# Three stage seams of a decoder step: embedding rows turned tile by tile, the convolution state turned in the decode chain, the layer embeddings loaded and split during the down projection

## The chip, the core and the metric

The kernel runs on one core of a Trainium2 chip. The core has TensorE (matrix products, into PSUM), VectorE, ScalarE and GpSimd (POOL), each with an instruction queue of its own that is worked off in order, and 16 DMA engines; SyncE (SP) issues most DMAs. Engines wait for each other by semaphores. The metric is device time in microseconds of one execution; lower is better.

## The reference

One inference step of a two-layer decoder trunk: 512 prompt tokens and 8 x 4 decode tokens share the weights, in all 544 tokens of width 1024.

```python
def trunk_layer(h, p, pos0, past, weights):
    a = rmsnorm(h, g_attn)
    qa, ka, va, qi, ki, wi, qb, kb, vb, u = split_columns(a @ w_in)
    ...                                   # three head groups: sparse, stick-breaking, pooling
    mix = jnp.concatenate([o_a, o_b.reshape(B, T, WIDTH_B), o_c], axis=-1)
    h = h + mix @ w_out
    y_ffn, new_conv = conv_ffn(rmsnorm(h, g_ffn), conv_prefix, w_up, conv_w, conv_b, w_down)
    h = h + y_ffn
    h = h + jax.nn.sigmoid(rmsnorm(h, g_ple) @ w_ple_gate) * (p @ w_ple_proj)
```

In `conv_ffn`, `f @ w_up` gives a gate and a value half of 2816 columns each; the gate goes through a causal convolution of width 3 over tokens (for decode tokens the two rows before come from `state_conv`), then SiLU, times the value, then `@ w_down`. `p` (256 wide) is a second input per token and layer, the layer embedding.

## The kernel before

Activations are kept with features on the partitions: `hT` is 8 blocks of 128 features by 544 tokens. Weights are streamed in **units** of 128 x 1024 numbers, 106 per layer: 12 and 8 for `w_in`, 8 for `w_out` (U_OUT), 44 for `w_up` (U_UP; gate and value by turns), 24 for `w_down` (U_DOWN, three per output block), 2 for `w_ple_proj` (U_PROJ), 8 for `w_ple_gate` (U_GATE). SP loads a unit into one of four raw buffers (`load_unit`, which waits for `w_lo` of the unit four before), ScalarE rounds it to `w_H` (`split`, which waits for `w_used`, that is, for the unit two before to be used), VectorE makes the rest `w_L` = raw - `w_H` and counts `w_lo`. TensorE then does every product as three (`tri_product`: high x high, low x high, high x low), and `dense` is one unit: 8 blocks of 6 matmuls with 272 token columns each.

`norm_block` on ScalarE makes the rounded, gain-scaled input (`aH` or `bH`) and the square of each hT block, `norm_low` on VectorE the low half (`aL`, `bL`), GpSimd adds up the squares, `square_sum` on TensorE sums them over the partitions with four fp32 matmuls (shown as eight), and `root` on ScalarE takes the inverse root with Ln and Exp, for which it loads tables.

What sets the order is the order in the program of each engine, written by hand. The places at issue:

- **Start.** SP loads the constants `con`, the mask, the page numbers, all four prompt tiles of `x_prompt` in one DMA and then `x_sample` into `xy`, then 12 small vectors, then the first four weight units. TensorE waits for both parts of `xy` and turns the 5 tiles (8 transposes each), VectorE copies them to `hT` (line 1170) and counts `h_new`. Then come the vectors' turn, the splits of two units and the first `norm_block`s.
- **Out to up projection.** `state_conv` is loaded to `st_tok` when the decode chain is done (line 592). After the last out unit TensorE turns it (line 2031, 22 transposes), does `square_sum(1)`, waits for ScalarE's copy to `stT` and enters the loop over up units. ScalarE's queue there holds the last splits and `norm_block(1, 7)`, the copy to `stT`, `root(1)`, and then the loop `ffn`: per gate block `split` of an even unit, the convolution steps, a sigmoid, `split` of the odd unit, and the rounding of the product. VectorE has the steps between; a block's odd unit is thus split only behind most of the convolution of that block.
- **Decode chain.** While VectorE picks the top keys, TensorE turns 16 key pages (line 1917) and forms logits; then it waits for ScalarE's and VectorE's softplus (line 1501) before the stick-breaking sums (line 1979) and the output products (lines 2005, 2016).
- **Down projection to embedding projection.** SP loads `p_tok` when the last down unit is used (line 602). TensorE turns it (line 2070, 10 transposes), ScalarE copies it as `pH`, VectorE makes `pL`, and the 8 blocks of the projection follow, with `square_sum(2)` behind the fourth. ScalarE moves each block to `projT`.

## Time and profile before

| | us |
|---|---|
| median of 3 runs | 1719.51 |
| lowest and highest | 1717.09, 1720.02 |
| the profiled execution | 1722.34 |
| its span in the profile | 1720.5 |
| TensorE busy | 1637.9 (95% of the span) |
| VectorE, ScalarE, GpSimd busy | 885.7, 681.6, 271.3 |
| mean granted clock of TensorE | 0.958 |

The profile is one execution. A granted clock of 1.00 is 2.4 GHz, one of 0.50 is 1.2 GHz. In rows of the timeline, the first number is the start, the second the duration, and the bracket holds the idle time of the engine ahead of the row and what ended it. Matmuls overlap in a pipeline, so the step from one start to the next, not the duration, is the time that one costs.

### The profile page before, as it was taken

The numbers are of one execution on the slowest core, as the hardware profiler recorded it, in microseconds if no ns is written. First come the engines' busy times: TensorE is split into PE (matmuls) and PEld (weight loads), VectorE is DVE, ScalarE is ACT, GpSimd is POOL, SyncE is SP. The second block draws the span as 40 slices with busy tenths as digits, with TensorE's granted clock in tenths as the row PEclk, the third lists the DMA queues.
The fourth block names the chain that finished last, engine by engine and source line by source line (L and its number), as shares of the span: only waits on it lengthen the run. The fifth ranks groups of instructions, "written<-read, shape, count | busy, mean of one in ns | idle before, by whom it ended". The sixth has DMA issues, their size and how long they took to land.

```text
span 1720.5 us, 31176 instructions
## 1 busy us (share of the span) xinstructions
PE 1637.9 (95%) x12030; PEld 1487.6 (86%) x12032; DVE 885.7 (51%) x1567; ACT 681.6 (40%) x981; POOL 271.3 (16%) x448
## 2 busy tenths in 40 slices
PE   5999979999999999998999999799999999999898
PEld 4787836799999999997978786369999999999898
DVE  5657884144555553322748488632355555522325
ACT  3344544235444442224443344532444444322241
POOL 2320240021111111000104105101111111100000
PEclk9999989699999999998999999888999999999989
DMA  5133142132223232332322311322232322233321
GB/s 163 51 95 81 32 134 74 30 86 74 85 85 98 79 89 80 89 92 75 86 75 79 103 48 55 94 66 69 72 89 85 94 85 85 80 92 89 98 61 57
DMA packets 225670, 140.07 MB, mean 81 GB/s; under 512 B 13074, under 2 KB 219684, under 8 KB 225504
## 3 DMA queue, kind: packets, MB, share of 16 engines
q1 hardware_dynamic: 223172, 133.32, 26.9%
q0 software_dynamic: 2400, 5.42, 1.0%
q8 instruction: 65, 1.06, 0.3%
q14 instruction: 33, 0.27, 0.1%
HBM read 131.06 MB, written 7.65 MB: 81 GB/s over the span
## 4 chain that ended last, share of the span: by engine, by line
PE 83%; DVE 10%; ACT 2%; issue 2%; DMA 1%; POOL 0%; DVEq 0%; SPq 0%; POOLq 0%; ACTq 0%
PE ps L1624 24%; PE ps L1626 23%; PE ps L1625 23%; DVE score L1285 2%; DVE m L1282 2%; PE ps L1930 1%; PE ps L2005 1%; PE ps L1687 1%; DVE w_L L1184 1%; PE ps L1773 1%; PE ps L1917 1%; PE ps L1873 1%; PE ps L1927 1%; DVE stat L1403 1%; PE ps L1651 1%
## 5 line engine op out<-in xcount | busy, mean ns | idle before, releaser
L1184 DVE TENSOR_TENSOR w_L<-w_raw,w_H 128x1024 fp32r<-128x1024 f32 (+4 forms) x236 | 257.3, 1099 | 443.7 <-ACT w_H L822 443.7
L1624 PE MATMUL ps<-bH,w_H 128*128 128x272 f32 x1664 | 481.9, 290 | 1.4 <-ACT projT L822 1.4
L1626 PE MATMUL ps<-bH,w_L 128*128 128x272 f32 x1664 | 480.2, 289 | 0.0
L1625 PE MATMUL ps<-bL,w_H 128*128 128x272 f32 x1664 | 478.5, 288 | 0.0
L822 ACT ACTIVATE w_H<-w_raw 128x1024 fp32r<-128x1024 f32 (+4 forms) x236 | 220.0, 943 | 298.6 <-PE ps L1626 298.3
L1624 PEld LDWEIGHTS ps<-bH,w_H 128*128 128x128 f32 x1664 | 313.5, 188 | 2.3 <-ACT projT L822 1.9
L1625 PEld LDWEIGHTS ps<-bL,w_H 128*128 128x128 f32 x1664 | 314.5, 189 | 0.2
L1626 PEld LDWEIGHTS ps<-bH,w_L 128*128 128x128 f32 x1664 | 313.4, 188 | 0.0
L1624 PE MATMUL ps<-actH,w_H 128*128 128x272 f32 x704 | 204.1, 290 | 0.0
L1626 PE MATMUL ps<-actH,w_L 128*128 128x272 f32 x704 | 203.7, 289 | 0.0
L1625 PE MATMUL ps<-actL,w_H 128*128 128x272 f32 x704 | 202.7, 288 | 0.0
L1624 PE MATMUL ps<-aH,w_H 128*128 128x272 f32 x512 | 153.5, 300 | 1.6 <-DVE aL L1190 1.6
L1626 PE MATMUL ps<-aH,w_L 128*128 128x272 f32 x512 | 149.4, 292 | 0.0
L1625 PE MATMUL ps<-aL,w_H 128*128 128x272 f32 x512 | 148.8, 291 | 0.0
L1625 PEld LDWEIGHTS ps<-actL,w_H 128*128 128x128 f32 x704 | 132.7, 189 | 0.0
L1624 PEld LDWEIGHTS ps<-actH,w_H 128*128 128x128 f32 x704 | 132.5, 188 | 0.0
L1626 PEld LDWEIGHTS ps<-actH,w_L 128*128 128x128 f32 x704 | 132.4, 188 | 0.0
L1624 PEld LDWEIGHTS ps<-aH,w_H 128*128 128x128 f32 x512 | 98.0, 191 | 14.1 <-issue 12.2
L1624 PE MATMUL ps<-w_H,aH 128*128 128x512 f32 (+5 forms) x240 | 92.8, 387 | 8.5 <-DVE aL L1196 4.9
L1625 PEld LDWEIGHTS ps<-aL,w_H 128*128 128x128 f32 x512 | 98.2, 192 | 0.0
L1626 PEld LDWEIGHTS ps<-aH,w_L 128*128 128x128 f32 x512 | 97.8, 191 | 0.0
L1625 PE MATMUL ps<-w_L,aH 128*128 128x512 f32 (+5 forms) x240 | 89.9, 375 | 0.0
(318 smaller groups left out, 2427.2 us busy)
## 6 DMA issues: line engine op xcount, KB each, us to landing
w_raw<-in_w_up SPq DMA_DIRECT2D x88, 512.0 KB, 3.8
w_raw<-in_w_down SPq DMA_DIRECT2D x32, 512.0 KB, 3.6
w_raw<-in_w_in SPq DMA_DIRECT2D x24, 512.0 KB, 4.9
w_raw<-in_w_ple_gate SPq DMA_DIRECT2D x16, 512.0 KB, 3.7
w_raw<-in_w_down SPq DMA_DIRECT2D x16, 384.0 KB, 3.2
w_raw<-in_w_out SPq DMA_DIRECT2D x16, 320.0 KB, 3.4
w_raw<-in_w_in SPq DMA_DIRECT2D x8, 452.0 KB, 3.5
w_raw<-in_w_in SPq DMA_DIRECT2D x8, 384.0 KB, 3.2
```

The costliest lines, as they stand in the source:

```text
L822: return act.activation(out, in_, ACT.Copy, scale=scale)
L1184: ins = dve.tensor_tensor(w_L[u % SPLIT][:, a:b], w_raw[raw_slot(l, u)][:, a:b], w_H[u % SPLIT][:, a:b].bitcast(F32), ALU.subtract)
L1282: dve.max(m8[:, :], sc).then_inc(dve_step, steps.step())
L1285: dve.match_replace(sc, m8[:, :], sc, TAKEN).then_inc(dve_step, steps.step())
L1403: dve.tensor_reduce(stat[:, s, 0, :], ps[:, SOFT_BANK[s]:SOFT_BANK[s] + 2, 0:P * (t + 1)], AX.X, ALU.max).then_inc(dve_step, steps.step())
L1624: pe.matmul(out, wh, xh, start=start, stop=False)
L1625: pe.matmul(out, wh, xl, start=False, stop=False)
L1626: return pe.matmul(out, wl, xh, start=False, stop=stop)
L1651: mm = pe.matmul(ps[:, SUM_BANK[i] + half, 0:HALF], mean, x[:, HALF * half:HALF * half + HALF], start=n == 0, stop=n == 1, skip_group_chec ...
L1687: pe.matmul(ps[:, 7, 0:P * (t + 1)], featT[rows, F_QI + e // 2, P * t:P * t + P], featT[rows, F_KI, 0:P * (t + 1)], start=True, stop=True) ...
L1773: pe.matmul(bz(h, i), featT[rows, F_KB + h // 2, P * i:P * i + P], featT[rows, F_QB + h // 2, P * i:TP], start=i != 3, stop=False, skip_gr ...
L1873: mm = pe.matmul(ps[HD * n:HD * n + HD, 4, 0:384], V[:, b, HD * n:HD * n + HD], probT[:, b, n, :, :], start=b == 0, stop=b == t, skip_grou ...
```

## The change

At the start the prompt tiles are loaded by four DMAs with a semaphore each, ahead of the mask, and TensorE waits tile by tile; VectorE casts the mask behind the copies. The load of `state_conv` waits for the last page turn instead of the decode chain's end, its turns stand ahead of the stick-breaking sums, and ScalarE's copy behind its copies of the turned probabilities. The first of the 11 turns of the up loop on TensorE is written out, with `square_sum(1)` behind its first unit. The load of `p_tok` is issued behind the fourth down unit's, its turns stand behind the sixth down block, ScalarE's and VectorE's parts one block later at most, in other PSUM banks and in SBUF that the convolution has left. Two matmuls that wrote zeros to two banks ahead of the down projection are gone.

```diff
-        p_tok = sb("p_tok", [P, TILES, PLE], F32, ple)
-        pH = sb("pH", [P, 2, T], F32R, ple)
-        pL = sb("pL", [P, 2, T], F32R, ple)
...
+        keepT = sb("keepT", [P, KF, 2 + 2 * NB], F32, ffn)
+        late = ExitStack()
+        p_tok = sb("p_tok", [P, TILES, PLE], F32, late)
+        pH = sb("pH", [P, 2, T], F32R, late)
+        pL = sb("pL", [P, 2, T], F32R, late)
+        late.close()
         stT = sb("stT", [P, KF, 2 * NB], F32, ffn)
-        keepT = sb("keepT", [P, KF, 2 + 2 * NB], F32, ffn)
...
+        con_ld, page_ld, con_cast = sg("con_ld"), sg("page_ld"), sg("con_cast")
+        x_ld = [sg(f"x_ld{t}") for t in range(TILES)]
...
-        PP_BANK, PROJ_BANK = [0, 1, 6], [0, 4, 6]
+        PP_BANK, PROJ_BANK = [2, 3, 1], [0, 4, 6]
...
             sp.dma_start(con[:], t_in["con"]).then_inc(con_ld, 16)
-            sp.dma_start(mask[:], t_in["dcon"][:, ND:]).then_inc(con_ld, 16)
+            for t in range(4):
+                sp.dma_start(xy[:, t, :], t_in["x_prompt"][0, P * t:P * t + P, :]).then_inc(x_ld[t], 16)
+            sp.dma_start(xy[0:TS, 4, :], t_in["x_sample"].rearrange("b s d -> (b s) d")).then_inc(x_ld[4], 16)
+            sp.dma_start(mask[:], t_in["dcon"][:, ND:]).then_inc(con_cast, 16)
             sp.dma_start(pages[:], t_in["page_table"].rearrange("b n -> (b n)").rearrange("(o n) -> o n", o=1)).then_inc(page_ld, 16)
-            sp.dma_start(xy[:, 0:4, :], t_in["x_prompt"].rearrange("o (t p) d -> p (o t) d", p=P)).then_inc(x_ld, 16)
-            sp.dma_start(xy[0:TS, 4, :], t_in["x_sample"].rearrange("b s d -> (b s) d")).then_inc(x_ld, 16)
...
-                sp.wait_ge(d_hi, at(d_hi, 2))
+                sp.wait_ge(ik_sc, at(ik_sc, 1))
                 hold(sp)
-                sp.wait_ge(d_lo, at(d_lo, 2))
+                sp.wait_ge(kt_mm, at(kt_mm, NPAGES))
                 hold(sp)
                 sp.dma_start(st_tok[:], t_in["state_conv"][L].rearrange("o b r c -> (o b r) c")).then_inc(st_ld, 16)
...
-                for u in range(U_DOWN, U_PROJ + RAW):
+                for u in range(U_DOWN, U_DOWN + RAW):
                     load_unit(u)
-                sp.wait_ge(w_used, at(w_used, SPLIT + U_PROJ))
+                sp.wait_ge(s_mul, at(s_mul, KF))
+                hold(sp)
+                sp.wait_ge(g_keep, at(g_keep, KF))
                 hold(sp)
                 sp.dma_start(p_tok[:, 0:4, :], t_in["p_prompt"][L].rearrange("o b (t p) c -> p (o b t) c", p=P)).then_inc(p_ld, 16)
                 sp.dma_start(p_tok[0:TS, 4, :], t_in["p_sample"][L].rearrange("o b s c -> (o b s) c")).then_inc(p_ld, 16)
-                for u in range(U_PROJ + RAW, UNITS + (RAW if l + 1 < LAYERS else 0)):
...
+                act.wait_ge(st_tr, at(st_tr, 1))
+                copy(stT[:, :, :], ps[:, 4, 0:KF * 2 * NB].rearrange("p (f b) -> p f b", b=2 * NB)).then_inc(st_ev, 1)
                 act.wait_ge(vp_use, at(vp_use, NPAGES))
...
                     norm_block(1, m)
-                act.wait_ge(st_tr, at(st_tr, 1))
-                copy(stT[:, :, :], ps[:, 5, 0:KF * 2 * NB].rearrange("p (f b) -> p f b", b=2 * NB)).then_inc(st_ev, 1)
                 root(1)
...
+                def p_split():
+
+                    act.wait_ge(pp_tr, at(pp_tr, 1))
+                    for b in range(3):
+                        nt = 2 if b < 2 else 1
+                        src = ps[:, PP_BANK[b], 0:nt * 256].rearrange("p (t k q) -> p k t q", k=2, q=P)
...
+                        ins.then_inc(pp_hi, 1)
+
                 for m in range(KD):
                     for q in range(3):
                         split(U_DOWN + 3 * m + q + 2)
                     norm_block(2, m)
-
-                act.wait_ge(pp_tr, at(pp_tr, 1))
...
-                    ins.then_inc(pp_hi, 1)
+                    if m == 5:
+                        p_split()
+
...
-            dve.wait_ge(con_ld, 32)
+            dve.wait_ge(con_ld, 16)
...
-            dve.tensor_copy(con_bf[:, 1, :], mask[:, 0:P])
-            dve.tensor_copy(con_bf[:, 2, :], mask[:, P:2 * P]).then_inc(con_cast, 1)
             for t in range(TILES):
...
                     ins.then_inc((emb_ev if i < 2 else h_new), 1)
+            dve.wait_ge(con_cast, 16)
+            dve.tensor_copy(con_bf[:, 1, :], mask[:, 0:P])
+            dve.tensor_copy(con_bf[:, 2, :], mask[:, P:2 * P]).then_inc(con_cast, 1)
...
+                    if m == 6:
+                        p_low()
...
-            pe.wait_ge(con_ld, 32)
-            pe.wait_ge(x_ld, 32)
+            pe.wait_ge(con_ld, 16)
             for i in range(2 * TILES):
                 t, b, n = i // 2, i % 2, TOKW[i // 2]
+                if b == 0:
+                    pe.wait_ge(x_ld[t], 16)
                 if i >= 8:
                     pe.wait_ge(emb_ev, i - 7)
                 for k in range(4):
                     mm = pe.transpose(ps[:, i % 8, P * k:P * k + n], xy[0:n, t, P * (4 * b + k):P * (4 * b + k) + P], ident[0:n, 0:n])
                 mm.then_inc(emb_tr, 1)
-            pe.wait_ge(con_cast, 1)
+            pe.wait_ge(con_cast, 17)
...
+                pe.wait_ge(kt_ev, at(kt_ev, NPAGES))
+                pe.wait_ge(st_ld, at(st_ld, 16))
+                hold(pe)
+                for f in range(KF):
+                    mm = pe.transpose(ps[:, 4, 16 * f:16 * f + 16], st_tok[:, P * f:P * f + P], ident[0:16, 0:16])
+                mm.then_inc(st_tr, 1)
...
+                pe.wait_ge(st_ev, at(st_ev, 1))
                 pe.wait_ge(d_lo, at(d_lo, 2))
...
-                pe.wait_ge(st_ld, at(st_ld, 16))
-                pe.wait_ge(h_new, at(h_new, KD + 6))
-                hold(pe)
-                for f in range(KF):
-                    mm = pe.transpose(ps[:, 5, 16 * f:16 * f + 16], st_tok[:, P * f:P * f + P], ident[0:16, 0:16])
-                mm.then_inc(st_tr, 1)
-                square_sum(1)
-                pe.wait_ge(st_ev, at(st_ev, 1))
-                pe.wait_ge(h_new, at(h_new, KD + 7))
-                hold(pe)
-
-                with pe.Fori(0, KF // 2) as i:
+                def up(i, first=False):
+
                     for j in range(4):
                         n = 4 * i + j
                         pe.wait_ge(w_lo, at(w_lo, RAW + U_UP + n + 1))
-                        if j % 2 == 0:
+                        if j % 2 == 0 and not first:
                             pe.wait_ge(v_mul, at(v_mul, 2 * i + j // 2 + 1))
-                        if j == 3:
+                        if j == 3 and first:
                             pe.wait_ge(n_rec, at(n_rec, 2))
-                        dense(2 * j, j, range(KD), bH, bL, True, True, norm_=1 if j == 0 else None).then_inc(w_used, 1)
+                        if first and j < 3:
+                            pe.wait_ge(h_new, at(h_new, KD + (7, 8, 8)[j]))
+                        dense(2 * j, j, range(KD), bH, bL, True, True, norm_=1 if first and j == 0 else None).then_inc(w_used, 1)
+                        if first and j == 0:
+                            square_sum(1)
+
+                up(0, True)
+                with pe.Fori(1, KF // 2) as i:
+                    up(i)
 
                 pe.wait_ge(v_mul, at(v_mul, KF - 2 + 3))
                 hold(pe)
-                for b in range(2, 4):
-                    pe.matmul(ps[:, b, 0:HALF], con_bf[:, 3, :], con_bf[:, :, :].rearrange("p a n -> p (a n)")[:, 0:HALF], start=True, stop=True)
...
-
-                pe.wait_ge(p_ld, at(p_ld, 32))
-                pe.wait_ge(h_new, at(h_new, 3 * KD - 1))
-                hold(pe)
-                for t in range(TILES):
...
+                    if m == 5:
+                        pe.wait_ge(p_ld, at(p_ld, 32))
+                        pe.wait_ge(v_mul, at(v_mul, KF + 2))
+                        hold(pe)
+                        for t in range(TILES):
...
+                                mm = pe.transpose(ps[:, PP_BANK[t // 2], c:c + n], p_tok[0:n, t, P * k:P * k + P], ident[0:n, 0:n])
+                        mm.then_inc(pp_tr, 1)
+
                 pe.wait_ge(g_keep, at(g_keep, KF))
...
                             pe.wait_ge(pr_ev, at(pr_ev, m - 2))
+                        elif m == 0:
+                            pe.wait_ge(h_new, at(h_new, 3 * KD - 1))
                         elif m == 1:
                             pe.wait_ge(h_new, at(h_new, 3 * KD))
                         mm = dense(PROJ_BANK[m % 3], u, range(2), pH, pL, True, True, c0=P * mm_, stride=512)
```

How the instructions stand. TensorE, from the out projection (`aH`, `aL`) to the up projection (`bH`, `bL`), first before, then of the change:

```order
1506 L1626 MATMUL ps<-aH,w_L 128x272
1507 L2031 MATMUL ps<-con,st_tok 128x16 [waits st_ld,h_new]
1508 L2031 MATMUL ps<-con,st_tok 128x16 x21
1509 L1651 MATMUL ps<-r_all,con 128x272 [waits n_add]
1510 L1651 MATMUL ps<-r_all,con 128x272
1511 L1651 MATMUL ps<-a_tmp,con 128x272 [waits n_sq]
1512 L1651 MATMUL ps<-a_tmp,con 128x272
1513 L2038 UNCONDITIONAL_BRANCH [waits st_ev,h_new]
```

```order
1514 L1642 MATMUL ps<-aH,w_L 128x272
1515 L1640 MATMUL ps<-bH,w_H 128x272 [waits a_lo,h_new,w_lo]
...
1562 L1642 MATMUL ps<-bH,w_L 128x272
1563 L1667 MATMUL ps<-r_all,con 128x272 [waits n_add]
1564 L1667 MATMUL ps<-r_all,con 128x272
1565 L1667 MATMUL ps<-a_tmp,con 128x272 [waits n_sq]
1566 L1667 MATMUL ps<-a_tmp,con 128x272
1567 L1640 MATMUL ps<-bH,w_H 128x272 [waits h_new,w_lo]
```

The turns of `st_tok` are gone from here, and a whole unit of 48 matmuls stands between the out projection and the square sum.

TensorE, in the decode chain of the change, between the biased logits (`bias_d`) and the stick-breaking sums (`L_d`):

```order
1097 L1989 MATMUL ps<-bias_d,id_bf 96x288 [waits d_bias]
1098 L1989 MATMUL ps<-bias_d,id_bf 96x288
1099 L1995 MATMUL ps<-con,st_tok 128x16 [waits kt_ev,st_ld]
1100 L1995 MATMUL ps<-con,st_tok 128x16 x21
1101 L2001 MATMUL ps<-L_d,con 128x192 [waits d_sp]
1102 L2002 MATMUL ps<-L_n,con 128x192
```

Here the turns are new; before, the row of `L_d` stood right behind that of `bias_d`.

TensorE, around the turns of `p_tok`, first before (behind the last down unit), then of the change (behind the sixth of eight down blocks), and then where the embedding projection (`pH`, `pL`) begins:

```order
2771 L1626 MATMUL ps<-actH,w_L 128x272
2772 L2070 MATMUL ps<-con,p_tok 128x128 [waits p_ld,h_new]
2773 L2070 MATMUL ps<-con,p_tok 128x128 x7
2774 L2070 MATMUL ps<-con,p_tok 128x32 x2
2775 L1624 MATMUL ps<-pH,w_H 128x272 [waits w_lo,pp_lo,g_keep]
```

```order
2704 L2089 MATMUL ps<-con,p_tok 128x128 [waits p_ld,v_mul]
2705 L2089 MATMUL ps<-con,p_tok 128x128 x7
2706 L2089 MATMUL ps<-con,p_tok 128x32 x2
2707 L1640 MATMUL ps<-actH,w_H 128x272 [waits h_new,w_lo]
...
2970 L1642 MATMUL ps<-actH,w_L 128x272
2971 L1640 MATMUL ps<-pH,w_H 128x272 [waits w_lo,h_new,pp_lo,g_keep]
```

The projection now follows a down matmul directly, and the wait for `p_ld` stands two down blocks ahead of it.

## Rows read from the trace of the kernel before

**Rows 1.** The page, part 4: shares of the chain of waits.
```profile
PE 83%; DVE 10%; ACT 2%; issue 2%; DMA 1%; POOL 0%; DVEq 0%; SPq 0%; POOLq 0%; ACTq 0%
```
**Rows 2.** The chain of waits at the start: start us, us, what.
```profile
2.49 9.65 DMA xy<-in_x_sample
12.27 4.51 PE ps L1614 x20
16.81 2.89 DVE hT L1170 x6
...
25.14 0.79 PE ps L1624
```
**Rows 3.** Timeline, down projection to embedding projection, both layers.
```profile
791.29 0.71 DVE L1556 TENSOR_TENSOR hT<-hT,ps 128x544 f32<-128x544 f32 x1
793.43 2.29 PE L2070 MATMUL ps<-con,p_tok 128*128 128x128 f32 x10 [4.46 <-DMA p_tok<-in_p_sample]
798.03 0.56 PE L1624 MATMUL ps<-pH,w_H 128*128 128x272 f32 x1 [2.31 <-issue]
...
1634.06 2.29 PE L2070 MATMUL ps<-con,p_tok 128*128 128x128 f32 x10 [4.83 <-DMA p_tok<-in_p_sample]
```
**Rows 4.** The chain of waits: decode products, and square sums of both layers.
```profile
317.96 10.34 PE ps L2005 x192
...
805.96 1.83 PE ps L1651 x8
...
1647.71 1.83 PE ps L1651 x8
```
**Rows 5.** Stretches: PE busy, PEld, DVE, ACT, POOL, clock, DMA share, GB/s.
```profile
24.00:26.00 2.00, 0.86 (x2) 0.76 (x3) 2.00 (x3) 1.91 (x4) 1.64 (x1) 0.50 0.84 210
```
**Rows 6.** Tile w_raw, issues from 7.4 to 8 us: units one and two.
```profile
L509 SPq DMA_DIRECT2D w_raw<-in_w_in x2: 390/394/399, 7.1 to 7.6; - x2
...
DMA to landing us min/median/max: 6.7/7.2/7.6
```
**Rows 7.** Timeline, out projection to up projection, first layer.
```profile
383.71 1.53 PE L2031 MATMUL ps<-con,st_tok 16*128 16x16 f32 x22
383.88 1.06 ACT L822 ACTIVATE w_H<-w_raw 128x1024 fp32r<-128x1024 f32 x1 [1.77 <-PE ps L1626]
387.64 0.79 DVE L1196 SCALAR_TENSOR_TENSOR bL<-hT,vecT,bH 128x544 fp32r<-128x544 f32 x1
389.94 0.71 ACT L856 ACTIVATE r_all<-ps,con 128x544 f32<-128x544 f32 x1
...
392.65 1.28 ACT L822 ACT_TABLE_LOAD   x1
397.01 1.06 ACT L822 ACTIVATE w_H<-w_raw 128x1024 fp32r<-128x1024 f32 x1 [3.08 <-PE ps L1626]
...
405.61 1.22 DVE L1184 TENSOR_TENSOR w_L<-w_raw,w_H 128x1024 fp32r<-128x1024 f32 x1
409.04 1.06 ACT L822 ACTIVATE w_H<-w_raw 128x1024 fp32r<-128x1024 f32 x1 [0.79 <-PE ps L1626]
...
417.62 1.22 DVE L1184 TENSOR_TENSOR w_L<-w_raw,w_H 128x1024 fp32r<-128x1024 f32 x1
```
**Rows 8.** Timeline of the decode chain: last page turn, first stick-breaking sums.
```profile
303.11 0.64 PE L1917 MATMUL ps<-con,KPa 128*128 128x128 f32 x4
...
310.79 1.01 PE L1979 MATMUL ps<-L_d,con 128*128 128x192 f32 x2 [3.25 <-DVE L_n L1501]
```
**Rows 9.** Stretches around the decode gap, columns as in rows 5.
```profile
306.00:308.00 2.00, 1.54 (x22) 0.83 (x21) 0.42 (x1) 1.04 (x3) 0.00 (x0) 0.70 0.00 0
...
336.00:338.00 2.00, 2.00 (x13) 2.00 (x12) 0.00 (x0) 0.00 (x0) 0.00 (x0) 0.62 1.06 238
```
**Rows 10.** DMA issues from 330 to 340: count, KB each, us to landing.
```profile
st_tok<-in_state_conv SPq DMA_DIRECT2D x1, 176.0 KB, 3.6
```
**Rows 11.** Tile xy: landing times of its two loads.
```profile
DMA to landing us min/median/max: 8.4/9.0/9.7
```

More of the change, by code:

```diff
@@ L250, in build @@
         act_low = ExitStack()
[L251 removed]
+        sb("act_skip", [P, KF * T - DFF + 256], F32, act_low)
         st_tok = sb("st_tok", [2 * NB, DFF], F32, act_low)
@@ L603, in _ @@
                 sp.dma_start(p_tok[0:TS, 4, :], t_in["p_sample"][L].rearrange("o b s c -> (o b s) c")).then_inc(p_ld, 16)
-                for u in range(U_PROJ + RAW, UNITS + (RAW if l + 1 < LAYERS else 0)):
+                for u in range(U_DOWN + RAW, UNITS + (RAW if l + 1 < LAYERS else 0)):
                     load_unit(u)
@@ L1119, in _ @@
                     norm_block(2, m)
-                act.wait_ge(pp_tr, at(pp_tr, 1))
-                for b in range(3):
-                    nt = 2 if b < 2 else 1
-                    n = nt * P if b < 2 else TS
-                    src = ps[:, PP_BANK[b], 0:nt * 256].rearrange("p (t k q) -> p k t q", k=2, q=P)
-                    if b < 2:
-                        ins = copy(pH[:, :, 256 * b:256 * b + 256].rearrange("p k (t q) -> p k t q", q=P), src)
-                    else:
-                        ins = copy(pH[:, :, TP:T], ps[:, PP_BANK[b], 0:256].rearrange("p (k q) -> p k q", q=P)[:, :, 0:TS])
-                    ins.then_inc(pp_hi, 1)
+                    if m == 5:
+                        p_split()
                 for q in range(2):
@@ L1551, in _, with p_low @@
                         ffn(j, 2 * i + j, 2 * j, i)
+                def p_low():
+                    for b in range(3):
+                        dve.wait_ge(pp_hi, at(pp_hi, b + 1))
+                        if b < 2:
+                            q = slice(256 * b, 256 * b + 256)
+                            for k in range(2):
+                                ins = lo(pL[:, k, q].rearrange("p (t q) -> p t q", q=P),
+                                         ps[:, PP_BANK[b], :].rearrange("p (t k q) -> p k t q", k=2, q=P)[:, k],
+                                         pH[:, k, q].rearrange("p (t q) -> p t q", q=P))
+                        else:
+                            ins = lo(pL[:, :, TP:T], ps[:, PP_BANK[b], 0:256].rearrange("p (k q) -> p k q", q=P)[:, :, 0:TS], pH[:, :, TP:T])
+                        ins.then_inc(pp_lo, 1)
                 for m in range(KD):
```

25 lines of the change are left out of this document (7 added, 18 removed).

## The prediction

> **What bounds the kernel now.** I read the chain of waits first. TensorE holds 83% of it [rows 1], so the end moves only where TensorE waits or where its queue gets shorter. Then I read the chain and the timeline around each place that the change touches, and noted for each wait what came last.
>
> At the start TensorE waits for the last embedding row's load, which lands at 12.14 us; VectorE's copies into hT end at 19.70, and the first dense matmul starts at 25.14 [rows 2]. Two more places follow in each layer. After the down projection TensorE waits 4.46 us for p_tok's load (until 793.43), turns it, and waits 2.31 us for the split until 798.03 [rows 3]. The square sum behind the first projection unit comes only at 805.96 [rows 4]. Between the out projection and the up projection, near 384 us, it turns the convolution state and then waits for the last square. After such waits the granted clock is low: it is 0.50, which is 1.2 GHz, at the first dense matmuls [rows 5].
>
> **The start.** Tiles can now be turned as they land, so the eight big copies lie beside the loads. The same bytes are loaded in nearly the same order, so I keep 12.1 us for the last row block; behind it stand two small copies only, and hT is whole near 12.5 instead of 19.70. What is late next is the second weight unit: it is issued at 7.6 and lands 7.6 us later, at 15.2 [rows 6]. SP's three extra issues push its issue to about 9, but the DMA engines are then still at work on the embeddings, so I leave the landing. From 15.2 on there are w_H at 1.06, w_L at 1.22 and the first low half of the input at 0.79 [rows 7], with some 0.25 for the gaps: 18.5 instead of 25.14. **Gain 6.6.** The mask and its two casts hide ahead of that landing. The first matmuls stay at the low clock as before, since the idle time ahead of them is about as long. Bounds: 5.4, if the weights land 1.2 later along with their issue, and 7.3, if hT alone sets it.
>
> **Out to up projection.** The 22 turns leave this place, and the first dense unit is put ahead of the square sum. The out projection ends at 383.84, where ScalarE's next split is released. A unit needs 6.01 us (two take 409.04 - 397.01 = 12.03), or 0.75 per block. The unit's eighth block needs bL at 388.43 [rows 7] and is reached at 383.84 + 7 x 0.75 = 389.1, so it does not wait. The unit ends at 389.85, the square sum takes 1.83 at the high clock [rows 4] and ends at 391.7. Read naively, the second unit then starts 5.2 us sooner. But ScalarE has the root of the norm in its queue ahead of the third unit's split, and that takes from 389.94 to 393.93, 3.99 us with two table loads [rows 7]. So that split starts at about 395.75 against 397.01 before: 1.27 sooner only. Everything on the chain behind it keeps its distances. The third unit starts at 398.1, after a wait of 0.4, and ends at 404.1. The fourth needs its w_L, ready at 406.83 before [rows 7] and at 405.55 now: a new wait of 1.4 us. It started at 409.0 and starts now at 405.6. **Gain 3.4 per layer, 6.8 in all**, as the second layer shows the same pattern. Bounds 2.5 and 5.2 per layer. Later units catch up: from the w_H at 409.04, 9.8 us pass until the odd unit's w_L is ready at 418.84 [rows 7], and TensorE takes 12.0 for two units.
>
> **The turns in the decode chain.** They stand now in TensorE's gap, which ends at 310.79 [rows 8] and begins at 307.54 (TensorE is busy for 1.54 of the stretch from 306 to 308 [rows 9]). Their load waits for the last page turn, which ends at 303.75 [rows 8], and lands about 3.6 us after its issue [rows 10], near 307.6. The 22 turns took 1.53 at the high clock [rows 7]. Here the clock has fallen (0.70 on average from 306 to 308 [rows 9]), so I give them 2.6 to 3.0: they end at 310.2 to 310.6, just inside the gap. Queued behind them is the whole stick-breaking product and with it the output products. Cost between 0 and 0.7 per layer; **I take 0.3 in all**, since the end falls inside the gap. ScalarE's copy of the result hides beside 10.34 us of TensorE's products [rows 4]. SP no longer holds the last four loads for the out projection until the decode work ends; TensorE never waited for them, so that brings nothing.
>
> **Into the embedding projection.** Issuing p_tok's load before the down projection hides it. SP now waits at that place for the last convolution product, which holds up the fifth down unit's load by some 7 us; its split comes more than 10 us after that, so it is covered. The ten turns are in TensorE's queue behind the sixth down block and cost their own time: eight at up to 0.16, as the last page turn's four take 0.64 at the high clock [rows 8], and two small ones, with the 2.29 of the low clock as the upper bound [rows 3]. I take 1.3 per layer, 2.6 in all. ScalarE's three and VectorE's five split instructions, 2.3 us together, move into queues that are idle for most of each 16.7 us block. At the down projection's end the first projection block starts at once and takes 1.5. The second writes the PSUM bank of the last down block, whose add ends at 792.0 [rows 3], 3.0 after the end: a wait of 1.5 us is left there. Three more blocks end 7.6 us after the down projection, and there stands the square sum. It stood at 805.96 - 788.97 = 17.0 in the first layer and at 1647.71 - 1629.23 = 18.5 in the second [rows 3, 4]. What follows it (root, table loads, copies) waits for the same things as before, so gains of 9.4 and 10.9 stay: **20.3 less 2.6, 17.7**. Two filler matmuls per layer go as well, 0.5 in all at 0.125 each.
>
> **Sum.** 6.6 + 6.8 - 0.3 + 17.7 + 0.5 = 31.3 us. The profiled execution took 1722.34 (its span 1720.5) and would take 1691.0. The median before is 2.83 below it, so the forecast is 1719.51 - 31.3 = 1688.2.
>
> **Rivals.**
> 1. *The tiles land together.* If the DMA engines share the loads out between the tiles, turning tile by tile wins little: the big load lands at 2.04 + 8.4 = 10.4 [rows 11], the turns and copies behind it take 7.4 (12.27 to 19.70), and 5.4 stand behind those as before: 23.3, a gain of 1.8 at the start and 1693.0 in all. For it speaks that the small last load, issued 0.45 us behind the big one, lands 1.7 later. Chance 0.08. The Trainium skill (DMA: Bandwidth & Descriptors, Queues, rings and completion order) has each engine consume its ring in order, though writes may overtake one another; by it the tiles land one after another, and no row of this trace decides it.
> 2. *The clock falls in the wait of 1.5 us that is left* after the first projection block. From the first block to the square sum TensorE took 805.96 - 798.03 = 7.9 us, and in the second layer 9.0, where four blocks at the high clock are 6.0: 1.9 and 3.0 lost, 1693.1 in all. The wait is much shorter than the one before, which speaks against it. Chance 0.08.
> 3. *The turns bring the clock back up in the decode gap.* It is low from 306.8 until about 337.5 [rows 9]. With the products of 10.34 us and nearly all else that TensorE does there at twice the speed, that is up to 11.5 less per layer: 1665. Against it: the clock fell while TensorE was still issuing, ahead of the gap, and the 22 turns have 16 columns each. Chance 0.03. The Trainium skill (TensorE: Matmul & The Clock Gate, Part 4: PE-mode transpose) says that transposes do not count as busy in the way that matmuls do; by it this case is out.
> 4. *Slower: the up projection becomes bound by the chain of ScalarE and VectorE.* The loop now starts with that chain late instead of early. If a turn of it took longer than TensorE's 12.0 us for two units, each of the 44 turns of both layers would pay. It decides at 12.0 + 31.3 / 44 = 12.7 us, against the 9.8 read above; at 13.5 the loss is 66 less 31, so 1754. The loop's body is unchanged, which speaks against it. Chance 0.02.
>
> **Numbers.** The forecast holds 0.79, and by its own bounds reaches from 1683 to 1694: the start may give 1.2 less, the place before the up projection 1.8 less or 3.6 more, the turns of p_tok 2 less, the decode gap 1.1 less. Rivals 1 and 2 end at 1693, and with some of those losses at 1698. The range is 1683 to 1698. Some 0.2% (3.4 us) is what a measurement of this kernel can tell from no change: faster 0.96, same 0.02, slower 0.02.
>
> **What would show it.** Right: the first dense matmul at 18.5; no wait between the last out block and the first up block, one of 0.4 before the third and of 1.4 before the fourth up unit; the 22 turns ending before VectorE's L_n does; the square sum 7.6 us behind the down projection at a clock of 1.00. Wrong: weights that land after 17 us at the start, down units that wait for w_lo, TensorE idle behind st_tok's load, or a root that starts later than 0.1 us after its sum.

## The result and the profile after

The changed kernel takes 1689.21 us (median; 1687.11 to 1690.12) where the kernel before takes 1718.41 beside it: ratio 0.9821, 95% interval 0.9807 to 0.9835, so 28 to 33 us less. The forecast was 1688.2, range 1683 to 1698. The profiled execution took 1690.09 us (span 1688.3, mean clock 0.968) against 1722.34 (1720.5, 0.958) before. The spans of the two profiles differ by 32.2, against a forecast sum of 31.3; the medians differ by 29.2. The page's part 4, as in rows 1: TensorE holds the same share of a shorter chain.

```profile
PE 83%; DVE 11%; ACT 3%; issue 2%; POOL 0%; DMA 0%; DVEq 0%; SPq 0%; ACTq 0%; POOLq 0%
```

The total agrees better than its parts. Chain of waits, changed kernel, start (columns as in rows 2; tile 0 had landed at 5.1, the second lands with the first row; `con_bf` are the mask's casts, L1679 the vectors' turn, `vecT` its copies):

```profile
1.67 6.43 DMA xy<-in_x_prompt
...
8.14 5.40 PE ps L1630 x24
...
13.56 1.12 DVE hT L1178 x3
14.68 0.13 DVE con_bf L1182
14.82 0.15 DVE con_bf L1183
...
15.01 0.43 PE ps L1679 x2
...
15.62 0.27 ACT vecT L828
...
15.91 0.03 ACT w_H L828
...
17.09 1.70 DVE w_L L1195 x3
...
18.91 0.68 DVE w_L L1195
19.59 0.71 DVE aL L1207
...
20.34 0.79 PE ps L1640
```

The tiles do land one after another, but hT is whole only at 14.68, and the first dense matmul starts at 20.34, not 18.5: 4.8 us sooner than in rows 2. The second weight unit, issued at 10.0, landed 6.2 us later, at 16.2, and held nobody up: ScalarE reached its part only at 17.0. Tile w_raw, the issue at 10.0:

```profile
DMA to landing us min/median/max: 6.2/6.2/6.2
```

The decode gap and the way into the up projection, TensorE's timeline, first layer (in brackets: idle before, and what ended it):

```profile
301.07 2.50 PE L1995 MATMUL ps<-con,st_tok 16*128 16x16 f32 x22
304.56 1.01 PE L2001 MATMUL ps<-L_d,con 128*128 128x192 f32 x2 [1.00 <-DVE L_n L1512]
...
391.87 0.40 PE L1640 MATMUL ps<-bH,w_H 128*128 128x272 f32 x1 [0.40 <-DVE w_L L1195]
...
399.36 0.39 PE L1640 MATMUL ps<-bH,w_H 128*128 128x272 f32 x1 [1.21 <-DVE w_L L1195]
```

The turns end 1.00 us before L_n is there (rows 8). The two waits that the prediction named are there, 0.40 and 1.21. Into the embedding projection, first the timeline, then the chain of waits:

```profile
783.74 0.39 PE L1640 MATMUL ps<-pH,w_H 128*128 128x272 f32 x1 [1.59 <-DVE hT L1581]
```
```profile
746.04 1.11 PE ps L2089 x10
...
788.53 1.83 PE ps L1667 x8
...
1614.76 1.83 PE ps L1667 x8
```

The ten turns of p_tok run for 1.11 us inside the down projection and put off what follows by 1.30 (the down matmuls are 9.63 ahead of the kernel before's in front of them, 8.33 behind them); 1.59 us of waiting are left after the first projection block. The square sums stand at 788.53 and 1614.76, at full clock, where rows 4 have 805.96 and 1647.71.

By stage, from the times of the same instructions in both traces (changed kernel sooner by, us):

| stretch | gain | predicted |
|---|---|---|
| start, to the first dense matmul | 4.8 | 6.6 |
| clock up sooner behind it | 0.6 | - |
| clock near 243 and 270 us | 0.85 | - |
| decode gap, both layers | 0 | -0.3 |
| clock in the rest of the attention, layers one and two | -0.1, -0.3 | - |
| out to up, layers one and two | 3.2, 3.2 | 3.4, 3.4 |
| two filler matmuls less, both layers | 0.5 | 0.5 |
| embedding projection, layers one and two | 7.8, 9.3 | 8.1, 9.6 |
| entry of layer two | 3.1 | - |
| tail | -0.7 | - |

(The predicted 17.7 is split here over the layers. The 0.85 is the balance of two falls of the clock: the kernel before loses 1.7 us to one at 269 us, the changed kernel 0.85 to one at 243 us.) The entry of layer two is a gain nobody planned. The changed kernel's clock is 1.00 there throughout, while the kernel before has a stretch in which TensorE never pauses and the clock is near half (kernel before, stretches, columns as in rows 5):

```profile
870.00:874.00 4.00, 4.00 (x12) 2.70 (x11) 3.41 (x5) 1.78 (x3) 1.47 (x2) 0.57 0.44 126
```

### The profile page after: what moved, and what is told of

It is laid out like the page before. It is cut to its first block, busy times and chain, and to the rows that moved or that the text cites. A ratio compares the mean times of both kernels' runs of the same rounds, so it can differ in the third digit from the quotient of the medians.

```text
span 1688.3 us, 31122 instructions
## 1 busy us (share of the span) xinstructions
PE 1628.6 (96%) x12026; PEld 1480.4 (88%) x12028; DVE 886.3 (52%) x1567; ACT 681.0 (40%) x981; POOL 272.4 (16%) x448
## 3 DMA queue, kind: packets, MB, share of 16 engines
q8 instruction: 68, 1.11, 0.3%
## 4 chain that ended last, share of the span: by engine, by line
PE 83%; DVE 11%; ACT 3%; issue 2%; POOL 0%; DMA 0%; DVEq 0%; SPq 0%; ACTq 0%; POOLq 0%
PE ps L1640 23%; PE ps L1642 23%; PE ps L1641 23%; DVE score L1296 2%; DVE m L1293 2%; PE ps L1946 1%; DVE w_L L1195 1%; PE ps L2027 1%; PE ps L1703 1%; PE ps L1789 1%; PE ps L1933 1%; PE ps L1889 1%; PE ps L1943 1%; DVE Lb L1367 1%; PE ps L1667 1%
```

## The experiments

The runs come from five batches, each with the kernel before beside it. The time of the kernel before is in two groups, in one batch of 13 runs 1715.9 to 1718.8 (five) and 1722.2 to 1723.3 (eight), so a batch's median of it is anything from 1718.4 to 1722.2, and a stage's gain is read better from the traces than from two medians. The intervals of the four single edits (split first to splits before copies) overlap the changed kernel's, so what each of them brings rests on its profile alone; the interval of the four together doesn't overlap it.

| kernel | median us | before beside it | ratio, 95% interval | span of the profile |
|---|---|---|---|---|
| changed | 1689.21 | 1718.41 | 0.9821 [0.9807, 0.9835] | 1688.3 |
| start alone | 1712.10 | 1722.22 | 0.9953 [0.9939, 0.9967] | 1712.3 |
| projection undone | 1706.50 | 1722.22 | 0.9923 [0.9896, 0.9950] | 1705.7 |
| sum first | 1697.06 | 1722.22 | 0.9868 [0.9843, 0.9893] | 1694.8 |
| before again | 1716.78 | | | 1715.0 |
| split first | 1686.43 | 1718.50 | 0.9811 [0.9787, 0.9834] | 1684.9 |
| projection banks | 1687.98 | 1718.50 | 0.9815 [0.9797, 0.9832] | 1685.9 |
| start kept busy | 1687.36 | 1718.50 | 0.9821 [0.9797, 0.9845] | 1684.5 |
| splits before copies | 1687.85 | 1718.50 | 0.9818 [0.9798, 0.9839] | 1684.7 |
| turns twice | 1691.28 | 1718.85 | 0.9834 [0.9809, 0.9859] | 1691.0 |
| decode kept busy | 1703.27 | 1718.85 | 0.9917 [0.9889, 0.9945] | 1701.5 |
| four edits | 1680.99 | 1721.42 | 0.9771 [0.9753, 0.9788] | 1676.0 |
| four edits, gap kept busy | 1674.98 | 1721.42 | 0.9731 [0.9716, 0.9746] | 1673.2 |

**The start alone.** The hunks of the start put into the kernel before, nothing else.

> The kernel before with the start alone changed (token rows turned tile by tile). Theory: the first dense matmul comes 4.8 us sooner and the clock rises a little sooner after it, so 4.8 to 5.4 us in all, 1713.0 to 1713.6 where the kernel before takes 1718.4; a fall of the clock near 270 us, as the kernel before has it, may or may not show, worth 0.85. Rival, the sum of the prediction as it stood: 6.6 us, 1711.8. Rival, a sooner start only moves an idle stretch to a later wait: within 1 us of the kernel before.

The first dense matmul starts at 17.99 (TensorE's timeline):

```profile
4.93 4.57 PE L1618 MATMUL ps<-con,xy 128*128 128x128 f32 x24 [4.93 <-DMA xy<-in_x_prompt]
9.74 1.70 PE L1618 MATMUL ps<-con,xy 128*128 128x128 f32 x16 [0.24 <-DMA xy<-in_x_prompt]
12.68 0.39 PE L1667 MATMUL ps<-con,vec_raw 114*128 114x114 f32 x2 [1.24 <-DMA vec_raw<-in_conv_w]
17.99 0.79 PE L1628 MATMUL ps<-w_H,aH 128*128 128x512 f32 x1 [4.92 <-DVE aL L1199]
```

That is 7.2 sooner than in rows 2, with the same code that gave 4.8 in the changed kernel. In this execution the turns of 128 tokens start 0.21 us apart up to 8.6 us and 0.11 apart from there on, while in the changed kernel all 32 of them start 0.21 apart, the last at 13.1. Over the eight profiles whose start is the changed kernel's, the first dense matmul is at 17.99, 18.89, 18.97, 19.42, 19.43, 20.05, 20.32 and, in the changed kernel itself, 20.34; in two of the kernel before it is at 25.14 and 25.76. So the start is worth 4.8 to 7.8 by the execution, 6.0 on average of these, and the expectation's 4.8 to 5.4 took one late case for the rule. The whole run is 8.1 us faster by its ratio (5.7 to 10.5), which lies above the 4.8 to 5.4; the rival's 6.6 is within it. In all eight the way from the last copy into hT to the first dense matmul is 5.7 to 5.9 us. What decides is when TensorE turns at its faster pace: the later it takes it up, the later hT is whole (12.1 to 14.7) and the first dense matmul starts. The profile's clock column says 1.00 for the whole of this stretch, but 0.21 against 0.11 us for the same turn is the factor of two between 1.2 and 2.4 GHz.

**Projection undone, and the kernel before once more.** The changed kernel with the embedding rows loaded, turned and split after the down projection; and the kernel before, unchanged.

```
-    late = ExitStack(); p_tok, pH, pL = ...
-    turns and splits of p_tok inside the down projection
+    load p_tok, turn, split behind the down projection
```

> The changed kernel with the PLE seam as it was before: the embedding rows are loaded, turned and split after the down projection again; start, decode turns and the order of square sum and up units stay changed. Theory: the seam was worth 7.8 us in the first layer and 9.2 in the second, so this takes 1706 to 1707 where the changed kernel takes 1689.2. Rival, the 3.1 us that the changed kernel gained at the entry of the second layer, where the kernel before shows a clock at half for some us, also came from the seam: then 1709 to 1710, and the profile shows the fall of the clock near 870 and 890 us again.

> The kernel before, unchanged, for one more profile. In the one profile so far the granted clock falls to half near 270 us (first layer only) and near 870 and 890 us (entry of the second layer), in stretches in which TensorE works without a pause; the changed kernel shows 1.00 in all of them, which is 0.85 and 3.1 us of its gain that the prediction had not. Theory A, chance of one execution: the falls stand elsewhere or not at all here, and the span is up to 4 us below 1720.5. Theory B, they belong to the kernel before: they stand in the same places, within some us.

The profile without the new projection is at 8.2 us behind the changed kernel after the first layer's projection, at 11.3 by the second layer's entry, and 18.6 behind after the second projection, 17.4 at the end. It was 0.25 behind ahead of the first seam and 10.95 ahead of the second: 7.9 and 7.7 for the seams, and 3.1 again at the entry. The sum is the theory's (1706.50), the falls at the entry are the rival's (stretches):

```profile
860.00:864.00 4.00, 4.00 (x12) 2.65 (x11) 3.87 (x4) 2.55 (x5) 1.34 (x1) 0.59 0.33 86
...
880.00:884.00 4.00, 4.00 (x19) 3.29 (x18) 0.00 (x0) 2.89 (x6) 0.00 (x0) 0.65 0.00 0
```

The kernel before once more has one of its two (a fall that runs from 868.0 to 871.4 us), and none near 270 us, where the first profile had one:

```profile
866.00:870.00 4.00, 3.04 (x9) 1.99 (x10) 3.24 (x5) 2.69 (x5) 0.93 (x1) 0.75 0.35 49
870.00:874.00 4.00, 4.00 (x16) 2.90 (x16) 1.75 (x3) 0.45 (x1) 0.54 (x2) 0.82 0.66 178
```

Its span is 1715.0, 5.5 less. So the 0.85 near 270 us is chance: of the 14 profiles of this study 7 show a fall there, of either kind of kernel, and 3 of the other 7 (the changed kernel's is one) show one at 242 us instead. The entry of layer two bears out neither theory whole. All four profiles with the old projection seam lose 1.7 or 3.4 us there; of the ten with the new one, eight lose nothing and two lose 1.7. One of those two (the split-first kernel) at the same place:

```profile
848.00:852.00 4.00, 3.05 (x9) 2.00 (x10) 3.24 (x5) 2.71 (x5) 0.94 (x1) 0.75 0.29 39
```

The idle stretch ahead is the same with the fall and without it: TensorE waits 1.87 us last, for sig, in the kernel before and 1.91 in the changed and the split-first kernel. What the seam 60 us earlier does to the clock at this entry stays open.

**Sum first.** The changed kernel with the square sum ahead of the first up unit and one loop again; the turns stay in the decode gap.

```
-    up(0, True)                 # the sum stands behind its first unit
-    with pe.Fori(1, KF // 2) as i:
+    square_sum(1)
+    with pe.Fori(0, KF // 2) as i:
```

> The changed kernel with one thing put back: the square sum stands ahead of the first up unit again and the up loop is one loop; the turns of the convolution state stay in the decode chain. Theory: all of the gain of that seam, 3.4 and 3.2 us, comes from the first up unit's two projections covering the last column's way through VectorE and ScalarE, so this takes 1695.5 to 1696 where the changed kernel takes 1689.2. Rival, part of the gain comes from the turns no longer standing in that gap (22 turns of 0.11 to 0.13 us, 2.5 to 3.0 us a layer, if they had not been hidden there): then 1690 to 1692.

The span is 6.5 longer than the changed kernel's, 3.2 in each layer, and nothing is left of the seam's gain (the median, 1697.06, is 1 above the range expected). TensorE's timeline:

```profile
377.81 1.18 PE L1667 MATMUL ps<-r_all,con 128*128 128x272 f32 x4 [0.31 <-POOL r_all L658]
381.93 1.77 PE L1667 MATMUL ps<-a_tmp,con 128*128 128x272 f32 x4 [2.93 <-ACT a_tmp L847]
```

The out projection ends at 377.50 and the last squares are ready at 381.93, 4.4 us later; in rows 7 they are 4.5 behind the point at which the turns began. The 22 turns had been free there too. They were filler, and taking them away alone turns work into waiting. The clock falls behind that wait (0.57 from 382 to 386), as it did in the kernel before (0.73 from 390 to 394), and stays at 1.00 in the changed kernel: of the 3.2 us of a layer about half is the clock (the first two up units take 13.5 us in the kernel before, 12.03 at the high clock).

**Turns twice.**

```
+    for q in range(2):
         for f in range(KF):
             mm = pe.transpose(ps[:, 4, 16 * f:16 * f + 16], st_tok[...], ident[0:16, 0:16])
```

> The changed kernel with the 22 turns of the convolution state done twice (44 instructions, 5.0 to 5.3 us at 0.11 to 0.12 us each) in the gap of the decode chain. Theory: in the changed kernel TensorE waits 1.00 us more behind the 22 turns for the logits' sums, so 22 more of 2.5 us stick out by 1.5 us a layer and the kernel is 3.0 us slower, 1692.2 where the changed kernel takes 1689.2; the first 22 are free. Rival: the turns are already late for a part, since the chain behind them moved too: then the second 22 cost their whole 2.5 us a layer, 1694.2. Rival: with TensorE busy through the gap the clock doesn't fall there: faster by up to 15 us a layer.

TensorE's timeline:

```profile
301.79 4.84 PE L1996 MATMUL ps<-con,st_tok 16*128 16x16 f32 x44
306.56 1.01 PE L2002 MATMUL ps<-L_d,con 128*128 128x192 f32 x2
```

This execution runs 0.67 later ahead of the gap; the sums come 2.00 later than in the changed kernel, so the second 22 cost 1.33 in the first layer (1.73 in the second) and the first 22 nothing. The span is 2.7 longer, near the 3.0 expected. The clock fell as before; turns don't hold it up. The Trainium skill (TensorE: Matmul & The Clock Gate, Part 4: PE-mode transpose) has transposes not count as busy for the clock. This run agrees, though it can't tell that from their being small. The start doesn't fit it: in the run with the start alone TensorE had done nothing but turns, 128 columns wide, and yet they went from 0.21 us apart to 0.11 behind the eighteenth. There the measurement decides: at the start, turns did bring the faster pace.

**Split first.** ScalarE's and VectorE's split of the third up unit ahead of the root.

```
+    split(U_UP + 2, 0, 4)
     root(1)
```

> The changed kernel with the split of the third up unit put ahead of the root of the square sum on ScalarE and VectorE. Theory: the waits of TensorE for w_L before the third (0.40 us) and fourth (1.21 us) up unit come from the root standing ahead of that split in the queue (two table loads and a 1.28 us Exp), so both go and the kernel is 1.6 us a layer faster, 3.2 us in all: 1686.0 where the changed kernel takes 1689.2. Rival: the root comes 2 us later and the first products that need the factor wait instead for n_rec; then no gain or up to 1 us a layer lost, 1689 to 1691. Rival: the third and fourth unit's weights land late, and the waits stay under another name: no change.

No wait of TensorE is left from 384 to 412 us. The profile is 0.15 ahead of the changed kernel at the square sum (383.47) and 2.28 ahead at the next one (chain of waits, both layers; 788.53 and 1614.76 in the changed kernel):

```profile
786.25 1.83 PE ps L1675 x8
...
1612.47 1.83 PE ps L1675 x8
```

That is 2.1 in the first layer, 0.5 more than the two waits, and 2.1 again in the second; the root had indeed stood in front of a split that was wanted sooner. The median fell by 2.8 against the changed kernel's.

**Projection banks.**

```
-    PROJ_BANK = [0, 4, 6]
+    PROJ_BANK = [0, 6, 4]
-    elif m == 1: pe.wait_ge(h_new, at(h_new, 3 * KD))
+    elif m == 2: ...
```

> The changed kernel with the second and third block of the embedding projection in each other's PSUM banks, and the wait for the last column of the hidden state a block later. Theory: the wait of 1.59 us after the first block (the add of the down projection's last column frees its bank that late) goes, since the next block's bank is free and its work covers the add: 3.0 us in all, 1686.2 where the changed kernel takes 1689.2. Rival: the wait only moves to the third block, since this add ends 2.3 us after the down projection and a block covers 0.9 to 1.6 us of it: then at most half the gain, 1687.5.

Chain of waits:

```profile
782.46 0.64 DVE hT L1581
783.12 0.75 ACT bH L828
783.88 0.55 ACT a_tmp L847
784.42 0.52 ACT projT L828
784.98 0.39 PE ps L1640
```

From the down projection's last column to the square sum it is 1.17 us less a layer, not 1.6 and not the rival's half either. The third block starts some 0.2 late for the add, and the fourth some 0.2 late for the first block's copy, which now stands in ScalarE's queue behind bH and a_tmp.

**The start kept busy, and splits before copies.** 14 multiplications behind the vector turn; and ScalarE's first two splits ahead of its copies of the vectors.

```
     mm.then_inc(vec_tr, 1)
+    for q in range(14): pe.matmul(ps[:, 7, 0:512], con_bf[:, 3, :], con_bf[...], start=True, stop=True)
```
```
+    split(0); split(1)
     act.wait_ge(vec_tr, 1)
-    split(0); split(1)          # stood behind the copies of vecT
```

> The changed kernel with 14 multiplications without use (512 columns each, into a bank nobody reads) in TensorE's idle stretch between the start's turns and its first dense product. Theory: the clock granted after the first dense product is the low one because TensorE stood idle for 5 us ahead of it; filled, the high one comes sooner, and of the 3.4 us that the low clock costs there 1.7 to 3.4 go: 1685.8 to 1687.5 where the changed kernel takes 1689.2. Rival: the clock is low there because it starts so in every execution and rises only on a certain amount of work, and the 14 products lie in the way of the first dense one: no change, or up to 3 us slower.

> The changed kernel with ScalarE splitting the first two weight units ahead of its copies of the vector rows. Theory: after the change the start is bound by the second weight unit's split, whose weights landed 14.9 us in and whose ScalarE part began at 15.9 us behind those copies, so the first dense product comes about 1 us sooner and the kernel takes 1688.2 where the changed kernel takes 1689.2. Rival: the VectorE half of the split (1.7 us for three instructions, from 17.1 us) is bound by its own queue, not by ScalarE's: no change.

Kept busy (TensorE's timeline):

```profile
14.15 3.19 PE L1682 MATMUL ps<-con_bf 128*128 128x512 bf16 x13
19.23 0.50 PE L1640 MATMUL ps<-w_H,aH 128*128 128x512 f32 x1 [1.90 <-DVE aL L1207]
```

The dense matmuls run at full clock from the second one on (0.23 each, where the changed kernel's first nine take 0.43). The profile is 1.1 ahead at the first of them, as hT was whole 1.1 sooner in this execution, and 2.78 ahead at 41 us: 1.7 from the clock. The rival is out. With the splits first, VectorE's queue has only two low halves ahead of the input's when the second unit is there (chain of waits):

```profile
16.34 0.62 ACT w_H L828
...
16.99 1.12 DVE w_L L1195 x2
...
18.20 0.79 DVE aL L1207
```

ScalarE splits the first unit at 14.45, as it lands, where the changed kernel splits both from 15.91 on. The second unit lands at 15.8 here, and ScalarE takes it up at once; the landing now binds, and the first dense matmul follows 3.25 us behind it, at 19.03. (The 14.9 of the expectation is the landing of the first unit in the changed kernel; the second landed at 16.2.) From the last copy into hT it is 4.9 us, against 5.7 in the changed kernel: 0.8 gained, near the 1 expected; the other 0.5 by which this start is sooner is hT's. By 41 us only 0.2 is left, as the low clock lasted longer here.

**The decode stage kept busy.** 29 multiplications without use a layer: 4 ahead of the last two pages' logits, 9 around the turns in the gap, 16 among the products with V.

> The changed kernel with multiplications without use (512 columns of bf16 each, into a bank nobody reads) among the decode attention's products: 4 ahead of the last two pages' logits, 9 in the gap, and one behind each of the 16 pages in the product with V, 29 a layer. Rival of the prediction, once more: the granted clock is at half for some 31 us a layer in which TensorE runs small products; if what is missing is work, these keep it at 1.00, and of the 15.4 us a layer that half a clock costs there (the sum of one minus the granted clock over the stretch) up to all come back, less some 4.3 us for the 20 that no gap hides: up to 22 us in all, 1667. Theory: such a fall can't be had back so cheaply; the clock stays at half and each costs 0.43 us, 6 to 9 us a layer slower, 1701 to 1707.

```
+    if pg >= 14: 2 x pe.matmul(ps[:, 7, 0:512], ...)      # ahead of page_logits(pg)
     turns, with 4 of these ahead of them and 5 behind
+    pe.matmul(ps[:, 7, 0:512], ...)                       # behind each page's products with V
```

TensorE's timeline, and a stretch behind it:

```profile
306.10 0.59 PE L2008 MATMUL ps<-L_d,con 128*128 128x192 f32 x2
...
310.26 0.52 PE L2034 MATMUL ps<-A_d,VP 128*64 128x4 f32 x12
```
```profile
314.00:318.00 4.00, 3.53 (x41) 2.56 (x40) 0.00 (x0) 0.00 (x0) 0.00 (x0) 0.50 0.00 0
```

A loss of 13.2 in the span, the size that the theory gave, but the theory's reason holds for one half of the stretch only. The clock stayed at 1.00 through the gap and through the whole stick-breaking product, each pair at 0.59 where the changed kernel has 1.01, and fell 1.3 us into the product with V, in spite of a multiplication behind every 12 of its products. From the start of that product to the out projection it took 9.3 us longer than in the changed kernel, 0.6 for each of the 16 multiplications, and the clock stood at half all the same: they bought nothing. This led to the last pair.

**Four edits together, and with the gap kept busy.** The second has the first two hunks of the last diff (13 multiplications a layer), and not the third.

> The changed kernel with the four small edits together: third up unit's split ahead of the root, the projection's banks exchanged, 14 multiplications without use in the start's gap, the first two weight splits ahead of the vector copies. By the single profiles, against the changed kernel's: 2.1 us a layer from the split (offset 0.15 before that seam, 2.28 behind it), 1.2 us a layer from the banks, 1.7 us from the clock at the start and 1.1 to 1.3 us from its first dense product: 9.4 us in all, 1680 where the kernel before takes 1718.5. Rival: the falls of the clock of 1.7 us each, which come and go from kernel to kernel, eat some of it: 1680 to 1685.

> The kernel with the four small edits, and of the decode multiplications without use only those ahead of the last two pages' logits (4) and in the gap (9), none in the product with V. Theory: these kept the clock at 1.00 until 311 us where it fell at 301 before; the sums and turns behind the gap took 0.5 to 0.6 us a pair where they took 1.0, and the first product with V began 1.7 us sooner although the gap ended 0.9 later; without the 16 in the product with V, which cost 0.6 us each at half the clock, 2 to 3 us a layer are gained: 4 to 6 us less than the kernel with the four edits alone. Rival: without the later ones the clock falls as early as it did, and the 4 ahead of the pages cost 0.9 us a layer: 2 us more than that kernel.

The four edits: 1680.99, the expected range. With the gap kept busy: 1674.98, 6.0 less, the upper end of what was expected. TensorE's timeline of the latter:

```profile
297.29 1.04 PE L2005 MATMUL ps<-con_bf 128*128 128x512 bf16 x4
298.26 1.53 PE L2010 MATMUL ps<-con,st_tok 16*128 16x16 f32 x22
299.72 1.25 PE L2013 MATMUL ps<-con_bf 128*128 128x512 bf16 x5
300.88 0.59 PE L2018 MATMUL ps<-L_d,con 128*128 128x192 f32 x2
...
305.04 1.97 PE L2044 MATMUL ps<-A_d,VP 128*64 128x4 f32 x48
306.86 2.71 PE L2044 MATMUL ps<-A_d,V 128*64 128x4 f32 x48
```

From the first stick-breaking sum (300.88) to the first page with V (305.04) it is 4.2 us; the changed kernel takes 7.1 (304.56 to 311.66). The clock falls near 306 and is back near 323, where it was low from 301 to 332: summed over the stretches, one minus the clock is 8.5 us a layer against 15.4 and 13.7. Against the four edits alone it is 0.3 ahead before the first layer's gap and 3.5 after it, and 1.15 and 4.3 in the second: 3.2 a layer. The 2.35 between them went at falls of the clock, one of 1.7 near 1081 us among them. Which of the 13 are needed, the 4 ahead of the pages or the 9 in the gap, was not tried. It is 14 us below the changed kernel by the medians, 46 below the kernel before (0.9731).

## Why the prediction was right

**The start, 6.6 forecast:** right in kind, and its size is within what the executions spread (4.8 to 7.8). In the profile of the changed kernel the term was 1.8 too large, and two steps of it failed. The first is "the eight big copies lie beside the loads" and "hT is whole near 12.5". Nothing there counts TensorE: when the second tile lands at 8.1, 24 turns of 128 tokens and 8 small ones are still to come, at 0.21 us for a big one, so hT was whole at 14.68, though the last row block had landed at 11.9 (forecast 12.1). The second is "What is late next is the second weight unit", at 15.2. It landed at 16.2, 1.0 later, and did not bind all the same. VectorE's casts of the mask, which were to hide, stand behind the last copy (0.28), the vectors' turn waits for them, and ScalarE's copies of the vectors hold its splits until 15.91. From hT to the first dense matmul it is 5.66, where rows 2 have 5.44: the start is set by hT and the chain behind it, which the prediction had only as its upper bound. The 3.3 from the landing on was right where the landing does bind, 3.25 with the splits ahead of the copies. Rival 1 is out: the five loads landed one after another, at 5.1, 8.1, 9.4, 11.5 and 11.9. The Trainium skill (DMA: Bandwidth & Descriptors, Queues, rings and completion order) has each engine consume its ring in order; this trace agrees.

**Out to up, 3.4:** measured 3.22 and 3.24, with the two waits where they were forecast (0.4 and 1.4 against 0.40 and 1.21), by the mechanism forecast: with the split ahead of the root both are gone. The working took both edits together; by the run with the sum first, all of the gain comes from the unit put ahead of the sum, and the turns' leaving gains nothing.

**The decode gap, 0.3:** 0. The turns began at 301.07 and took 2.50; forecast were 307.54 before, which is 301.3 in the changed kernel's time (6.23 sooner), and 2.6. Rival 3 is out as it was put: these turns of 16 columns don't hold the clock. That it was priced at all proved useful; nine products of 512 columns in the gap and four ahead of it together do hold it, until the product with V.

**The projection, 17.7 and 0.5:** measured 17.1 and 0.5 in the profile. The turns of p_tok cost the 1.3 a layer that were forecast, the wait of 1.5 was 1.59, and the square sum stands 7.9 behind the down projection, not 7.6: that is the 0.6 less. Rival 2 is out, the clock is 1.00 from 778 to 792 us. Undone, the seams cost 7.9 and 7.7: the 1.6 less in the second layer is how long the clock stays low behind the old seam, 6.8 us lost in the kernel before and 5.1 here.

**What was missing:** 3.1 us at the entry of layer two, 0.85 near 243 and 270 us and 0.6 behind the start, less 0.7 in the tail and 0.4 in the attention: 3.4 in all, and all of it the clock. Against it stand 1.8 that the start lacked, 0.4 of the way into the up projection and 0.6 of the projection, less the 0.3 that the decode gap didn't cost: 2.5. So the sum came within 1 us of the difference of the two profiles with errors of 3.4 and 2.5 us against each other. The mechanism was forecast rightly everywhere but at the start; that the sum came so close was luck, and by the medians it is 2.1 too large.

Rival 4 never came near: TensorE waits for nothing in the up loop behind its fourth unit.

## What to carry over

Work that fills a wait is free and taking it away gains nothing; what gains is to put other work of the queue into the wait, and to ask which queue the released work then meets (here the norm's root stood ahead of a weight split that was needed sooner). After a wait, count the clock with it: about half of what the way into the up projection gained was a fall that no longer came. And where small products follow a gap, a few large ones without use inside the gap can pay (here 13 a layer brought 3.2 us in each), but only up to the stretch that lets the clock fall anyway.

## What the hardware showed

- Turns of 128 columns at the start came 0.21 us apart at first and 0.11 later within one execution (the start alone), with nothing but turns on TensorE, under a clock column that says 1.00 throughout: before the first dense work, durations tell the clock, that column doesn't.
- Short falls of the clock come and go, for one kernel too: the same 16 products near 265 us take 2.80 us in seven profiles and 4.4 to 4.5 in the other seven. The two profiles of the kernel before differ by 5.5 us of span (1720.5 and 1715.0), and one minus the clock, summed over both, by 6.9; in the batch of 13 the medians of the two groups of its times lie 5.0 apart.
- The clock fell to half in the product with V, whose products have 4 columns, although TensorE was hardly idle: with the gap kept busy it was busy for 5.9 of the 6 us ahead of the fall at 306 us. One product of 512 columns behind every 12 of them (decode kept busy) didn't stop it.
